# A two-block mixer network on one core: the arena's base on 64 bytes, down products that wait by tile, and keys ahead of the root in the first mixer

## What is computed

```python
h = rms_norm(x, norm1_g) * (1 + sc1) + sh1
x = x + g1 * mixer(h)
h2 = rms_norm(x, norm2_g) * (1 + sc2) + sh2
gate, up = split(h2 @ w_ffn_in)              # 1024 -> 2 x 2816
x = x + g2 * ((silu(gate) * up) @ w_ffn_out) # 2816 -> 1024
```

```python
y = o * rsqrt(mean(o * o) + 1e-6) * norm_g * gate
```

## Time and profile before

| | |
|---|---|
| three runs | median 3044.2 us (3043.77 to 3046.67) |
| the profiled execution's own time | 3045.66 us |
| its span | 3043.9 us |
| mean granted clock of TensorE | 0.975 of 2.4 GHz |
| weights and constants read | 302.58 MB, 101 GB/s over the span |
| idle time of TensorE before lane products of mixer a (line 2335) | 35.4 us |

### The profile page before, as it was taken

One profiled execution on the slowest core, in us unless ns is written; L12 is line 12 of the kernel. 1 busy time (PEld: TensorE's weight loads), 2 busy tenths in 40 slices (PEclk: granted clock), 3 DMA queues, 4 the chain that ended last, 5 costly groups with the idle time before them and its releaser, 6 DMA issues.

```text
span 3043.9 us, 36720 instructions
## 1 busy us (share of the span) xinstructions
PE 2848.7 (94%) x15602; PEld 2249.3 (74%) x15602; DVE 1400.2 (46%) x1791; ACT 1103.0 (36%) x1339; POOL 232.2 (8%) x203
## 2 busy tenths in 40 slices
PE   6998989999989899999989999989899999899998
PEld 4875867887867677677778878777675777688876
DVE  5474555443455554345554443445443244533322
ACT  4374233222144432435432221344324454332222
POOL 1011311000020100011010000010100100100001
PEclk9998999999999999999999999999999999999999
DMA  8430014433331132122233433321231211322221
GB/s 317 153 145 15 4 46 156 152 138 118 131 111 56 49 123 110 65 106 88 91 133 139 150 136 137 104 73 56 80 118 42 86 56 44 123 81 99 94 87 56
DMA packets 46943, 309.68 MB, mean 102 GB/s; under 512 B 5531, under 2 KB 6427, under 8 KB 13500
## 3 DMA queue, kind: packets, MB, share of 16 engines
q1 hardware_dynamic: 44684, 297.33, 27.1%
q0 software_dynamic: 2096, 10.00, 0.9%
HBM read 302.58 MB, written 4.72 MB: 101 GB/s over the span
## 4 chain that ended last, share of the span: by engine, by line
PE 84%; ACT 7%; DVE 5%; issue 2%; DMA 1%; SPq 0%; ACTq 0%; POOL 0%; DVEq 0%
PE bank L2045 64%; PE bank L1985 5%; PE bank L2335 3%; PE bank L2145 2%; PE bank L2034 2%; PE bank L2355 2%; ACT WH L893 1%; DMA raw<-in_wstream_dram 1%; PE bank L2479 1%; PE bank L2346 1%; PE bank L2474 1%; ACT L958 1%; DVE WL L1399 1%; PE bank L2371 1%; PE bank L2107 0%
## 5 line engine op out<-in xcount | busy, mean ns | idle before, releaser
L2045 PE MATMUL bank<-HH,WH 128*128 128x512 f32 x2304 | 932.5, 405 | 61.5 <-DVE HL L1475 47.8
L2045 PE MATMUL bank<-HL,WH 128*128 128x512 f32 x2304 | 908.4, 394 | 0.0
L2045 PE MATMUL bank<-HH,WL 128*128 128x512 f32 x2304 | 907.5, 394 | 0.0
L1399 DVE TENSOR_TENSOR WL<-raw,WH 128x2048 fp32r<-128x2048 f32 (+2 forms) x263 | 490.7, 1866 | 708.7 <-ACT WH L893 707.6
L2045 PEld LDWEIGHTS bank<-HH,WH 128*128 128x128 f32 x2304 | 438.3, 190 | 181.5 <-issue 71.6
L893 ACT ACTIVATE WH<-raw 128x2048 fp32r<-128x2048 f32 (+3 forms) x223 | 395.7, 1775 | 411.5 <-PE bank L2045 396.6
L2045 PEld LDWEIGHTS bank<-HL,WH 128*128 128x128 f32 x2304 | 437.8, 190 | 95.9 <-issue 6.5
L2045 PEld LDWEIGHTS bank<-HH,WL 128*128 128x128 f32 x2304 | 437.2, 190 | 96.2
L2045 PE MATMUL bank<-AH,WH 128*128 128x512 f32 x492 | 195.2, 397 | 8.6 <-DVE AL L1519 8.6
L2045 PE MATMUL bank<-AL,WH 128*128 128x512 f32 x492 | 194.8, 396 | 0.0
L2045 PE MATMUL bank<-AH,WL 128*128 128x512 f32 x492 | 194.8, 396 | 0.0
(11 more groups left out here) (345 smaller groups left out, 3303.9 us busy)
## 6 DMA issues: line engine op xcount, KB each, us to landing
raw<-in_wstream_dram SPq DMA_DIRECT2D x256, 1024.0 KB, 4.8
raw<-in_wstream_dram SPq DMA_DIRECT2D x24, 512.0 KB, 3.5
raw<-in_wstream_dram SPq DMA_DIRECT2D x12, 768.0 KB, 4.2
bgam<-in_consts_dram POOLq DMA_DIRECT2D x2, 1792.0 KB, 7.0
bias_dram<-bias_row POOLq DMA_DIRECT2D x8, 320.0 KB, 6.6
xT<-in_x_dram SPq DMA_DIRECT2D x2, 1024.0 KB, 8.4
toep<-bias_dram POOLq DMA_DIRECT2D x8, 256.0 KB, 3.4
out_dram<-ost SPq DMA_DIRECT2D x4, 512.0 KB, 2.7
```

The costliest lines, as they stand in the source:

```text
L1399: TT(WL[:, wi % 2, now], raw[:, j.load % RAW, now], WH[:, wi % 2, now].bitcast(F32), ALU.subtract).then_inc(s["w_split"], 2 if half is Non ...
L2045: last = MM(o[m][0:cw, :], a, b, start=j.first and u == 0 and q == 0, stop=j.last and u == j.units - 1 and q == 2)
```

## The change

The arena's base is rounded up to a multiple of 64 bytes. Down jobs wait for the tiles that they read (8, 16 or 22 of the layer). ScalarE's root and YH copy of units 0 to 2 of mixer a move out of `finish` into the next unit (`head_root` behind the score copy of level 0, `head_high` behind the keys of level 2), and VectorE's two steps into levels 1 and 2 of its `scan` (`head_scaled`, `head_low`). In mixers a and c the keys of level 1 are taken ahead of the score copy of level 0. VectorE waits for `lanes` level by level, and before level 1 for product 0, which reads KK.

```diff
--- before.py
+++ after.py
@@ -381,7 +381,7 @@
         eps = sb("eps", [1])
         small = sb("small", [8, 4])
         table_col = sb("table_col", [1])
-        ARENA = base[0]
+        ARENA = (base[0] + 63) // 64 * 64
 
         def arena(name, kb, shape, dt=F32):
             off = ARENA + int(round(kb * 1024))
@@ -1275,16 +1275,26 @@
                     else:
                         A(sq, b0[:, :], ACT.Square).then_inc(s["h_sq"], 1)
                 ready_ln()
+                if st[1] == "a" and st[3] < 3:
+                    return
                 for x, (e, y) in enumerate(heads_):
-                    sq, rr, tt = temps[x]
-                    act.wait_ge(s["h_sum"], hd + x + 1)
-                    A(rr, bank[5 + 2 * e][:, :], ACT.Ln, bias=eps[:, :], scale=1.0 / P).then_inc(s["h_ln"], 1)
-                    act.wait_ge(s["h_ln"], hd + x + 1)
-                    A(rr, rr, ACT.Exp, scale=-0.5).then_inc(s["h_r"], 1)
+                    head_root(temps[x], hd + x, e)
                 for x, (e, y) in enumerate(heads_):
-                    act.wait_ge(s["h_y"], hd + x + 1)
-                    act.wait_ge(s["gemm_done"], GB[0])
-                    A(YH[:, y, :], temps[x][2], ACT.Copy).then_inc(s["h_high"], 1)
+                    head_high(temps[x], hd + x, y, GB[0])
+
+            def head_root(temps, hd, e):
+
+                sq, rr, tt = temps
+                act.wait_ge(s["h_sum"], hd + 1)
+                A(rr, bank[5 + 2 * e][:, :], ACT.Ln, bias=eps[:, :], scale=1.0 / P).then_inc(s["h_ln"], 1)
+                act.wait_ge(s["h_ln"], hd + 1)
+                A(rr, rr, ACT.Exp, scale=-0.5).then_inc(s["h_r"], 1)
+
+            def head_high(temps, hd, y, gemms):
+
+                act.wait_ge(s["h_y"], hd + 1)
+                act.wait_ge(s["gemm_done"], gemms)
+                A(YH[:, y, :], temps[2], ACT.Copy).then_inc(s["h_high"], 1)
 
             GB, ADDS = [0], [0]
             nrm = 0
@@ -1374,12 +1384,19 @@
                         a = aslot[i % 2]
                         hs, KK, KS = [(i % 2, a["ST"])], a["KK"], a["KS"]
                         act.wait_ge(s["prep"], 3 * forgets(st))
+                    later = kind == "a" and i > 0
                     for level in range(10):
+                        if level == 0:
+                            lane_keys(u, KK, KS[:, :], 1)
                         if level in (0, 8, 9):
                             for e, ST in hs:
                                 copy_scores(u, e, ST, level)
-                        if level < 7:
+                        if later and level == 0:
+                            head_root(own, hd - 1, (i - 1) % 2)
+                        if 0 < level < 7:
                             lane_keys(u, KK, KS[:, :], level + 1)
+                        if later and level == 1:
+                            head_high(own, hd - 1, i - 1, gemm_before(STEPS.index(("mix", kind, layer, i - 1))))
                         fill(st, level)
                     fill(st, 10)
                     finish(st, [(e, (2 * i + x) if kind == "c" else i) for x, (e, ST) in enumerate(hs)], hd, False)
@@ -1800,9 +1817,11 @@
 
                 sc0 = 7 * scan_before[st]
                 fill(st, 0)
-                dve.wait_ge(s["lanes"], 8 * u + 8)
                 for level in range(1, 9):
                     b = 2 ** (level - 1)
+                    dve.wait_ge(s["lanes"], 8 * u + level)
+                    if level == 1:
+                        dve.wait_ge(s["levels"], 10 * u + 1)
                     if level > 1:
                         dve.wait_ge(s["decayed"], 16 * u + 2 * (level - 1))
                     if level < 8:
@@ -1824,9 +1843,25 @@
                                                 bc(masks[:, level - 1, :], [0, 4], [1, P]),
                                                 bank[4 + 2 * e + level % 2][:, :].rearrange("p (j t) -> p j t", j=4)
                                                 ).then_inc(s["scores_put"], 1)
+                    if st[1] == "a" and st[3] > 0 and level == 1:
+                        head_scaled(st, hd - 1)
+                    if st[1] == "a" and st[3] > 0 and level == 2:
+                        head_low(st, hd - 1, st[3] - 1)
                     fill(st, level)
                 fill(st, 9)
                 fill(st, 10)
+
+            def head_scaled(st, hd):
+
+                sq, rr, tt = TEMPS[st[1]][0]
+                dve.wait_ge(s["h_r"], hd + 1)
+                dve.wait_ge(s["h_t"], hd + 1)
+                TT(tt, tt, rr, ALU.mult).then_inc(s["h_y"], 1)
+
+            def head_low(st, hd, y):
+
+                dve.wait_ge(s["h_high"], hd + 1)
+                TT(YL[:, y, :], TEMPS[st[1]][0][2], YH[:, y, :].bitcast(F32), ALU.subtract).then_inc(s["h_low"], 1)
 
             def finish(st, heads_, hd, group, layer):
 
@@ -2006,7 +2043,7 @@
                     if X[0] is YH:
                         pe.wait_ge(s["h_low"], heads_done(n))
                     elif X[0] is AH:
-                        pe.wait_ge(s["f_low"], 22 * (layer + 1))
+                        pe.wait_ge(s["f_low"], 22 * layer + min(k0 + 8, 22))
                 if kind in TOKEN_MAJOR:
                     for t in now:
                         if wd == CW:
```

## The result

| | before | after |
|---|---|---|
| median of four runs | 3045.43 us | 3002.63 us |
| profiled execution, own time | 3045.66 us | 3001.68 us |
| its span | 3043.9 us | 2999.9 us |
| mean granted clock | 0.975 | 0.982 |

The ratio is 0.986, 95% interval [0.9845, 0.9876]: 42.8 us less. The prediction was 3000.4 us, range 2992 to 3013. Lines are numbered anew in the changed kernel: 2045 is 2082, 2335 is 2372, 2034 is 2071.

What follows compares the result with a forecast made beforehand. TensorE, busy 94% of the span, was taken as the bound. Base 11.2, down products 9.9 and mixers 22.7 us sum to 43.8 us, taking the median of 3044.2 to 3000.4 us, range 2992 to 3013.

Steps and rivals of the forecast that it cites:

- the base changes nothing: Rival on the arena's base: that part does not do what it says, 3011.6 us, chance 0.12.
- 241.42 / 1056 = 228.6 ns with HH and HL: Pitch of uninterrupted wide matmuls with HH and HL moving, set against 233.8 ns with AH and AL.
- HH and HL start on a multiple of 64 bytes: Claimed difference in place from AH and AL, in an arena 32 bytes past one; 5.2 ns on 2160 matmuls.
- The cover: At down starts: 48 matmuls, 11.0 us, were to hide 8 us of VectorE work before the next part.
- units 0 to 1 and 1 to 2: First mixers, two layers: four transitions were to give 5.4 us, between 2.0 and 9.
- unit 2 to 3: First mixers: product 4 at 1070.0 against 1075.63; 5.6 us a layer, 11.2 in all, between 7 and 14.
- third mixers: Keys ahead of two score copies: 0.65 us before the second product, 0.5 for the second unit; 2.3 us over four units.
- I charge half: Units 0 to 2 of first mixers: half of 1.7 us for a lower-clock restart before product 2, 0.85 us each.
- The rival of 3009 us: First mixers: the wait only moves before product 2, with restarts at 1.2 GHz; mixer part gives 14 us; chance 0.20.
- From there fills cover: First mixers, unit 3: after product 4, filling matmuls were to hide further waits.
- last rival: First mixers: waits over products 2, 3 and 4 keep TensorE at its lower clock through fills; 3060 us, chance 0.02.
- slower rival: First mixers: fills at the lower clock, 0.20 us more a matmul, 60 us at 300 of them; chance 0.02.

Runs made afterwards that it cites:

- e1: The kernel before with the arena's base rounded up to 64 bytes and nothing else: 3036.69 us against 3044.59, ratio 0.9974.
- e11: The changed kernel with first-mixer weight splits of units 1 to 3 behind the second keys, and the arena's base rounded up to 128 bytes: 3003.47 us.
- e13: The changed kernel with first-mixer weight splits of units 1 to 3 behind the second keys, and everything from HH on 64 bytes further: 2996.27 us.
- e5: The changed kernel with 32 bytes of padding ahead of HH and behind HL: 3042.04 us, ratio 0.9989.
- e12: The changed kernel with AH's tiles 2080 bytes apart in place of 2048: 3004.31 us, ratio 0.9866.
- e2: The kernel before with the down products' wait by tile and nothing else: 3034.13 us, ratio 0.9965.
- e3: The changed kernel with the arena's base and the down waits undone, so the mixer part alone: 3026.51 us, ratio 0.9936.
- e6: The changed kernel with 32 bytes of padding ahead of WH and behind WL: 3046.15 us, ratio 1.0004.
- e10: The changed kernel with HH, HL and WH, WL all 32 bytes past a multiple of 64: 3046.09 us, ratio 1.0001.
- e9: The changed kernel with weight splits of units 1 to 3 behind second keys; in unit 3, slot-1 splits at level 4, YL difference behind level 5: 2996.76 us.
- e4: The mixer part alone on the kernel before, with root, YH copy and VectorE's two steps back in `finish`: 3043.32 us, ratio 0.9993.

## Why the prediction was right, and where it was off

**The base** was taken at 11.2 us and gave 7.9 (e1). It does shorten AH's and YH's matmuls, and the rival "the base changes nothing" fell. But the step "241.42 / 1056 = 228.6 ns with HH and HL" was wrong, as that piece starts with matmuls at 1.2 GHz. Inside it, in the kernel before, two starts 441 matmuls apart lie 99.96 us apart, 226.7 ns each:

```profile
1620.01 0.39 PE L2045 MATMUL bank<-HH,WH 128*128 128x512 f32 x1
...
1719.97 0.39 PE L2045 MATMUL bank<-HH,WH 128*128 128x512 f32 x1
```

And AH did not come down to HH's pitch but to 228.9, from 233.3: 4.4 ns in place of 5.2, on 1584 matmuls 7.0 us. YH's matmuls, in the mean over some 390 starts that follow on one another, went from 233.3 to 229.5 ns in e1, 2.2 us on 576. That is 9.2 us together, inside e1's interval (4.9 to 11.3 us). The reason put forward, "HH and HL start on a multiple of 64 bytes", fell with e11. What fits e11 and e13 is that AH then stood 64 and not 32 bytes from WH; e5 and e12 show that this is not all of it. That the 32 bytes helped is shown, why is not: the place was picked by a rule that doesn't hold, and this part of the gain was luck. The Trainium skill, SBUF — State Buffer, Specifications (TRN2), gives lines of 16 bytes; by that alone no shift here would have changed a read. Shifts of 32 and 64 bytes changed the time by 7.9 and 6.6 us, and the measurement decides. A shift of 16 bytes wasn't tried, so the size of a line stays open.

**The down waits**, 9.9 us with the clock, gave 10.5 (e2), 9.7 by the three pieces. The cover held: no wait shows at the down starts.

**The mixers**, 22.7 us, gave 18.1 by e3's times. The two kernels run the same 15602 matmul instructions in the same order, so starts can be compared one by one, and after's profile gives 22.8 us. That these meet is luck in part, as four misses cancel:

| part of the sum | said | measured, layers 1 and 2 |
|---|---|---|
| unit 0 | 0.6 + 3.2 | 0.4 + 2.8 us |
| units 0 to 1 and 1 to 2 | 5.4 in four | 2.0, 1.8, 1.9, 1.6: 7.2 us |
| unit 2 to 3 | 11.2 | 5.4 + 3.6 us |
| third mixers | 2.3 | 1.2 + 2.1 us |

Units 0 to 1, layer 1: from product 0 to product 2 it took 9.49 us for 11.51, 2.0 us won (2.2 to 2.3 said). The waits before product 2 are 1.56 to 1.62 us (up to 2 said), and none of the four was followed by the lower clock: here "I charge half", 0.85 us each, was mis-sized and should have been nothing. The rival of 3009 us needed those falls. It was near: waits of 1.97 to 2.00 us, before product 1 in the kernel before, were followed by 1.2 GHz four times in four. Waits of 1.48 to 1.62 us before product 2 were not in e3, e5, e6, e10 and e12 either, so none of 24 with after's.

Unit 2 to 3, counted from product 0: in layer 1 product 1 came 6.67 us earlier (6.8 said), product 4 at 13.8 us behind product 0 in place of 19.3, so 5.5 us (5.6 said). In layer 2 product 4 had won 5.3 us, but then 1.6 us went at 1.2 GHz, behind a wait of 1.25 us: "From there fills cover" left the clock out. That is the last rival's mechanism, at 1.6 us and not 60, and it isn't there each time: e3, e11, e12 and e13 have the wait and not the fall.

Third mixers: product 2 waits 1.65 us in place of 1.88, so 0.2 us and not the 0.65 said, but 0.5 us of waiting before product 1 went too, in each layer. 1.6 us more came in layer 2, where the kernel before had fallen to 1.2 GHz behind a wait of 1.74 us and after had not, behind the same wait. That is luck.

**Table loads**: "two more (one per layer)" was wrong. There are four more, as the gates of unit 3 load their table and the root loads the logarithm's again, in both layers (1343 instructions for 1339). The times of products 1 to 4 had counted both loads of a layer, so the sum was not off by it.

**The sum** of 43.8 us met 42.8 by the medians, 44.0 by the spans of the two profiled executions. The stages of the profile: feed-forward 17.1 us (9.9 + 1584 x 5.2 ns = 18.1 said), first mixers 19.9 (20.4 said), the rest of layers 1 and 2 6.1 (5.3 said), everything ahead of the first feed-forward part 0.9 (nothing said). The slower rival's price never showed: the clock rose in both windows. Stages that an edit leaves alone differ between two profiled executions by up to 3 us (what lies ahead of the first feed-forward part took 3.0 us longer in e9 than before), so single stages that agree within that say little.

## What to carry to other kernels

Read the pitch between starts in mid-stream for every pair of stationary and moving operands, and try another place for one of them where a pair is slower than the rest. Here 32 bytes on one pair cost 40 us. Neither alignment to 64 bytes nor the distance of the two told the pitch in every case, so measure the layout that you choose. Divide a piece of the chain by its count only after you have looked at its first matmuls. Where a wait is taken away, follow the queue of the engine that ends the next one: keys ahead of the root paid, and the split standing ahead of the second keys held back another 6 us.

## What the hardware showed unexpectedly

- 512-column fp32r matmuls stream at three pitches here where all tiles of an operand stand alike, 226.7, 228.9 and 233.3 ns (544, 549 and 560 cycles of 2.4 GHz), constant over 100 us. Stationary and moving operands both take part.
- Where the 512-column matmuls got slower by placement, the 256-column ones got faster: 119.9 ns at distance 0, 116.8 at -32 (e5, e6), 117.7 at -64 (e10, 96 in 11.30 us).
- The same instructions at the same addresses ran at 228.9 ns in one layer and 233.3 in two others (e5), and at 234.8 ns in the first column block and 229.2 in the other three of each layer (tile 3 in e12).
- The clock doesn't fall behind the same wait each time. Idle times of 1.96 to 2.00 us in the first mixers were followed by 1.2 GHz four times in four in the kernel before and in e2, but twice in four in e1. The 2.86 us ahead of down products: once in three in the kernel before and in e1, twice in three in e3 and e4. The 1.88 us of the earlier trace rows: never in the kernel before, once in two in e1 and in e2.
- Idle times of 1.41 to 1.65 us in the mixers of after and e4 were not followed by the lower clock. Two smaller ones were: the 1.58 us of the earlier trace rows, soon behind one of 1.18, and 1.16 and 1.25 us in unit 3 of layer 2 of after. I have no rule for it.
